# First products ordered by operand at two heads, and the norms' factors loaded in the program's first part

## The reference, cut to what matters

```python
def rms_norm(x, g):
    xf = x.astype(jnp.float32)
    y = xf * lax.rsqrt(jnp.mean(xf * xf, axis=-1, keepdims=True) + EPS)
    return (y * g.astype(jnp.float32)).astype(x.dtype)

def first_block(x, norm_pre, norm_post, ...):
    for i in range(DEPTH):
        h = rms_norm(x, norm_pre[i])
        ...
        x = x + rms_norm(y, norm_post[i])
    return x
```

## Time and profile before

| | us |
|---|---|
| median of three runs | 3822.8 |
| lowest and highest | 3817.92 and 3824.0 |
| the profiled execution's own time | 3820.23 |
| its span, first to last instruction | 3818.7 |
| PE busy | 3637.5 (95%) |
| DVE busy | 1873.1 (49%) |
| ACT busy | 1238.3 (32%) |

### The profile page before, as it was taken

One profiled execution on the slowest core, in us unless ns is written; L12 is line 12 of the kernel. 1 busy time (PEld: TensorE's weight loads), 2 busy tenths in 40 slices (PEclk: granted clock), 3 DMA queues, 4 the chain that ended last, 5 costly groups with the idle time before them and its releaser, 6 DMA issues. The chain is left out here.

```text
span 3818.7 us, 48925 instructions
## 1 busy us (share of the span) xinstructions
PE 3637.5 (95%) x18270; PEld 2939.1 (77%) x18270; DVE 1873.1 (49%) x3663; ACT 1238.3 (32%) x2411; POOL 130.8 (3%) x142
## 2 busy tenths in 40 slices
PE   8999999989999999999998899999958999999999
PEld 6888888857777777777777687677947777887887
DVE  4244244363333454555555544544675657644443
ACT  3243123133323333332323434443232333233222
POOL 0000010000000000000000100000010000000000
PEclk9999999999999999999999999999979999999999
DMA  4222242221111212211111320111222322232223
GB/s 144 98 85 66 64 130 69 88 91 58 52 57 38 73 54 63 58 53 46 45 46 50 112 107 26 40 48 57 87 104 89 100 80 86 73 113 94 99 94 121
DMA packets 134070, 292.16 MB, mean 77 GB/s; under 512 B 31217, under 2 KB 69665, under 8 KB 133777
## 3 DMA queue, kind: packets, MB, share of 16 engines
q1 hardware_dynamic: 117024, 248.03, 19.7%
q0 software_dynamic: 14768, 33.49, 2.9%
q10 hardware_dynamic: 2112, 8.39, 0.6%
HBM read 244.23 MB, written 51.85 MB: 78 GB/s over the span
## 5 line engine op out<-in xcount | busy, mean ns | idle before, releaser
L142 DVE TENSOR_TENSOR all_w_lo<-all_w_raw,all_w_hi 128x1024 fp32r<-128x1024 f32 x311 | 380.6, 1224 | 293.1 <-ACT all_w_hi L137 292.4
L137 ACT ACTIVATE all_w_hi<-all_w_raw 128x1024 fp32r<-128x1024 f32 x311 | 326.7, 1051 | 508.2 <-PE om_z L152 261.4
L1076 PE MATMUL da_z<-all_hi,all_w_hi 128*128 128x512 f32 x736 | 305.7, 415 | 4.1 <-DVE all_w_lo L142 4.1
L1076 PE MATMUL da_z<-all_hi,all_w_lo 128*128 128x512 f32 x736 | 291.3, 396 | 0.0
L1076 PE MATMUL da_z<-all_lo,all_w_hi 128*128 128x512 f32 x736 | 289.8, 394 | 0.0
L152 PE MATMUL om_z<-all_hi,all_w_hi 128*128 128x512 f32 x640 | 257.2, 402 | 7.5 <-DVE all_w_lo L142 4.4
L945 ACT ACTIVATE da_pt<-da_tr 128x512 f32<-128x512 f32 (+1 forms) x192 | 101.0, 526 | 486.3 <-PE da_tr L1129 486.3
L152 PE MATMUL om_z<-all_hi,all_w_lo 128*128 128x512 f32 x640 | 255.4, 399 | 0.0
L953 ACT ACTIVATE at_p<-at_logit,da_pair_max 128x256 f32<-128x256 f32 (+1 forms) x384 | 178.0, 465 | 238.4 <-DVE da_pair_max L1332 238.1
L152 PE MATMUL om_z<-all_lo,all_w_hi 128*128 128x512 f32 x640 | 253.7, 396 | 0.0
L152 PE MATMUL pr_g<-all_hi,all_w_hi 128*128 128x344 f32 (+1 forms) x624 | 212.2, 340 | 10.3 <-issue 4.9
(11 more groups left out here) (569 smaller groups left out, 7509.4 us busy)
## 6 DMA issues: line engine op xcount, KB each, us to landing
all_w_raw<-in_w_mlp SPq DMA_DIRECT2D x128, 512.0 KB, 3.4
all_w_raw<-in_w_ug SPq DMA_DIRECT2D x48, 512.0 KB, 4.2
all_w_raw<-in_w_qkv SPq DMA_DIRECT2D x48, 512.0 KB, 3.6
all_w_raw<-in_w_in SPq DMA_DIRECT2D x27, 512.0 KB, 3.6
da_w_raw<-in_w_qkv SPq DMA_DIRECT2D x24, 512.0 KB, 3.5
all_w_raw<-in_w_bo SPq DMA_DIRECT2D x24, 512.0 KB, 3.4
all_w_raw<-in_w_v SPq DMA_DIRECT2D x20, 512.0 KB, 4.0
vhat<-ag_vst ACTq DMA_DIRECT2D x4, 2048.0 KB, 7.3
```

Of the source, the lines that this page charges most:

```text
L137: self.nc.scalar.activation(self.hi[b][:, :], self.raw[b][:, :], ACT.Copy).then_inc(self.hi_done[b], 1)
L142: self.nc.vector.tensor_tensor(self.lo[b][:, :], self.raw[b][:, :], self.hi[b][:, :].bitcast(F32), ALU.subtract).then_inc(self.lo_done[b], 1)
L1076: last = nc.tensor.matmul(z[h][:, :], wp[u][:, ws], ap[:, kk, cols], start=(kk == 0 and m == 0), stop=(kk == KT - 1 and m == 2))
```

## The change

Three things. In ag, the first 12 products (k = 0 of unit 0) are ordered by operand: first the four with both upper halves, after a wait for `w_hi` and `hi[0]` only; then the four with `w_lo`; then the four with `lo[0]`. In da the 12 products of k = 0 of the first two weight units are ordered the same way, followed by the 6 of the third. And the four factor tiles `post0`, `pre1`, `post1`, `pre2` are kept for the whole program and loaded by SP in ag, behind `ln_b`, with a wait of SP for their landing; the four loads at the heads of da and pr and the waits for them are gone.

```diff
@@ gmlp, sync
             sp.dma_start(ln_b[:, :], a["ln_b"].rearrange("(j p) -> p j", p=P), allow_slow_non_contiguous=True).then_inc(s_lnp, 16)
+            for name, t in norms.items():
+                sp.dma_start(t, a[name]).then_inc(s_norms, 16)
+            sp.wait_ge(s_norms, 16 * len(norms))
             for u in range(2, len(v_units)):
                 load_v(u)
@@ gmlp, tensor
+                w.upper(pe, b, n)
+                wk = [t[b][:, :].rearrange("p (u k f) -> p k u f", u=4, k=2) for t in (w.hi, w.lo)]
+                if u == 0:
+                    pe.wait_ge(s_hi, 1)
+                    for m in ms:
+                        nc.tensor.matmul(bank[m][:, :], hi[:, 0, m * P:m * P + P], wk[0][:, 0], start=True, stop=False)
                 w.split(pe, b, n)
-                wk = [t[b][:, :].rearrange("p (u k f) -> p k u f", u=4, k=2) for t in (w.hi, w.lo)]
                 for k2 in range(2):
                     k = 2 * kp + k2
+                    if k == 0 and u == 0:
+                        for m in ms:
+                            nc.tensor.matmul(bank[m][:, :], hi[:, 0, m * P:m * P + P], wk[1][:, 0], start=False, stop=False)
+                        pe.wait_ge(s_lo, 1)
+                        for m in ms:
+                            nc.tensor.matmul(bank[m][:, :], lo[:, 0, m * P:m * P + P], wk[0][:, 0], start=False, stop=False)
+                        continue
@@ dilated_attention, sync
-            sp.dma_start(post[:, :], a_in["post0"]).then_inc(s_gain, 16)
-            sp.dma_start(pre[:, :], a_in["pre1"]).then_inc(s_gain, 16)
@@ dilated_attention, scalar; vector has the same
-            act.wait_ge(s_gain, 32)
@@ dilated_attention, tensor
+            pe.wait_ge(s_hi, 1)
+            for u in range(2):
+                w.split(pe, u, 0)
+            for m, (wp, ap) in enumerate(((w.hi, hi), (w.lo, hi), (w.hi, lo))):
+                if m == 2:
+                    pe.wait_ge(s_lo, 1)
+                for u in range(2):
+                    for h in range(2):
+                        nc.tensor.matmul(first[u][h][:, :], wp[u][:, 0:P], ap[:, 0, halves[h]], start=m == 0, stop=False)
+            w.split(pe, 2, 0)
             for k in range(KT):
                 pe.wait_ge(s_lo, k + 1)
-                for u in range(3):
-                    if k == 0:
-                        w.split(pe, u, 0)
+                for u in (range(3) if k else (2,)):
@@ projection_and_sticks, sync
-            sp.dma_start(post[:, :], a["post1"]).then_inc(s_norm, 16)
-            sp.dma_start(pre[:, :], a["pre2"]).then_inc(s_norm, 16)
@@ projection_and_sticks, scalar; vector has the same
-            act.wait_ge(s_norm, 32)
@@ the whole program
+        norms = {n: top.sb(n, [P, KT])[:, :] for n in ("post0", "pre1", "post1", "pre2")}
```

More of the change, by code:

```diff
@@ L146, in split, with upper @@
         pe.wait_ge(self.lo_done[b], self.uses[b] + n + 1)
+    def upper(self, pe, b, n):
+        pe.wait_ge(self.hi_done[b], self.uses[b] + n + 1)
     def products(self, out, b, act_hi, act_lo, cols, ks=range(KT)):
@@ L177, in over_same_bytes, with gmlp @@
         return t
-def gmlp(nc, a, w, hi, lo, x_kept, inv, vhat, vecs, tiles, ident, ones, yo):
+def gmlp(nc, a, w, hi, lo, x_kept, inv, vhat, vecs, tiles, ident, ones, yo, norms):
     heads, down = A_HEADS // 2, KT // 2
@@ L678, in attention_tiles, with dilated_attention @@
         return q, k_, v, bias, logit, p
-def dilated_attention(nc, a_in, w, hi, lo, x_kept, yo, over_yo, inv, inv_post, x_out, bias_dram, o_dram, lse_dram, lead, lead_sum, ident, ones):
+def dilated_attention(nc, a_in, w, hi, lo, x_kept, yo, over_yo, inv, inv_post, x_out, bias_dram, o_dram, lse_dram, lead, lead_sum, ident, ones, post, pre):
     turns = 3 * B_PAIRS
@@ L707, in dilated_attention @@
         pt.append(st.sb("pt1", [P, 512]))
-        post = st.sb("post", [P, KT])
-        pre = st.sb("pre", [P, KT])
         eps = st.sb("eps", [P, 1])
@@ L741, in dilated_attention @@
             st.sem(x) for x in ("qs", "vt", "vts", "qk_s", "max", "exp", "t", "pt_s", "pv_s", "rden_s", "o_s", "keep", "bias_s", "odma", "zero", "l", "ldma"))
-        s_free, s_ident, s_gain, s_eps, s_m, s_xp, s_hi, s_lo, s_sq, s_acc, s_tot, s_ln, s_inv, s_kept = (
-            st.sem(x) for x in ("gate_read", "ident_in", "gain_in", "eps_s", "m_s", "xp", "hi_s", "lo_s", "sq_s", "acc_s", "tot_s", "ln_s", "inv_s", "kept"))
+        s_free, s_ident, s_eps, s_m, s_xp, s_hi, s_lo, s_sq, s_acc, s_tot, s_ln, s_inv, s_kept = (
+            st.sem(x) for x in ("gate_read", "ident_in", "eps_s", "m_s", "xp", "hi_s", "lo_s", "sq_s", "acc_s", "tot_s", "ln_s", "inv_s", "kept"))
         s_lnd, s_share, s_lns, s_merge, s_before, s_stored, s_turned, s_yt = (
@@ L1672, in over_x_tiles, with projection_and_sticks @@
     return vt, dt, sd
-def projection_and_sticks(nc, a, w, hi, lo, inv, x, x_again, x_out, over_x, keep, table, cst, proj, conv, o_cat, ident, ones):
+def projection_and_sticks(nc, a, w, hi, lo, inv, x, x_again, x_out, over_x, keep, table, cst, proj, conv, o_cat, ident, ones, norms):
     units = [U_SQ, U_SK, U_SV, U_SQ + 1, U_SK + 1, U_SV + 1, U_DT] + list(range(U_X, U_X + 8)) + [U_Z, U_Z + 1, U_Z + 2, U_Z + 3,
@@ L1726, in projection_and_sticks @@
         gains = st.sb("gains", [P, 2])
-        post = st.sb("post", [P, KT])
-        pre = st.sb("pre", [P, KT])
+        post, pre = norms["post1"], norms["pre2"]
         eps = st.sb("eps", [P, 1])
@@ L1745, in projection_and_sticks @@
         begin = (g, [zb[0], zb[1], ob[0]])
-        (s_norm, s_par, s_table, s_m, s_xp, s_hi, s_lo, s_sq, s_acc0, s_tot, s_ln, s_inv, s_eps, s_zero, s_zout) = (
-            st.sem(n) for n in ("norm", "par", "table_in", "m_s", "xp", "hi_s", "lo_s", "sq_s", "acc0", "tot_s", "ln_s", "inv_s", "eps_s", "zero_s", "zero_out"))
+        (s_par, s_table, s_m, s_xp, s_hi, s_lo, s_sq, s_acc0, s_tot, s_ln, s_inv, s_eps, s_zero, s_zout) = (
+            st.sem(n) for n in ("par", "table_in", "m_s", "xp", "hi_s", "lo_s", "sq_s", "acc0", "tot_s", "ln_s", "inv_s", "eps_s", "zero_s", "zero_out"))
         (s_mm, s_ev, s_psq, s_blk, s_pb, s_r, s_nrm, s_vt, s_cm, s_cx, s_cl, s_ce, s_out, s_cc) = (
@@ L3095, in build @@
         x = yo = top.sb("yo", [P, KT, T])
-        gmlp(nc, a, w, hi_t, lo_t, x_kept, inv_t, vhat, vecs, tiles, ident, ones, yo)
+        gmlp(nc, a, w, hi_t, lo_t, x_kept, inv_t, vhat, vecs, tiles, ident, ones, yo, norms)
         with Stage(nc, "mixers") as st:
@@ L3100, in build @@
             x_again = dilated_attention(nc, a, w, hi_t, lo_t, x_kept, yo, over_yo, inv_t, inv[:, META:], x_dram, tiles, o_dram, lse_dram, lead,
-                                        lead_sum[:, :], ident, ones)
+                                        lead_sum[:, :], ident, ones, norms["post0"], norms["pre1"])
             c = st.sb("cst", [P, total - late])
@@ L3105, in build @@
             keep = {name: st.sb(name, shape).ap() for name, shape in shapes.items()}
-            projection_and_sticks(nc, a, w, hi, lo, inv, x, x_again, x_dram, over_x, keep, (c[:, :], a["cst"][:, late:total]), cst, proj, conv, o_cat, ident, ones)
+            projection_and_sticks(nc, a, w, hi, lo, inv, x, x_again, x_dram, over_x, keep, (c[:, :], a["cst"][:, late:total]), cst, proj, conv, o_cat, ident, ones,
+                                  norms)
             gated_recurrence(nc, proj, a["hg_gain"], cst, keep, FIRST, hi_f, x, x_dram, o_cat)
```

3 lines of the change are left out of this document (1 added, 2 removed).

## The result

| | before | after |
|---|---|---|
| median of 15 runs, us | 3826.29 | 3831.6 |
| lowest and highest | 3817.92 and 3831.33 | 3828.79 and 3836.09 |
| the profiled execution's own time | 3820.23 | 3831.74 |
| its span | 3818.7 | 3830.2 |

The ratio of the change to before is 1.0017, interval 1.001 to 1.0025: slower by 6.5 us (3.8 to 9.6); the two medians alone differ by 5.3. Of the miss of 9.4 us, 3.5 are the baseline: I anchored on the median of three runs, 3822.8, and the median of fifteen is 3826.29.

The account below looks back on a forecast made before the run. PE, busy 95% of the span, was taken as the bound, so edits pay only where it idles. Terms +2.5 (ag) - 2.35 (da) - 0.7 (pr) = -0.55 us against the 3822.8 us median gave 3822.2 us, range 3817 to 3828.

Parts of the forecast that it names:

- The order of products: Heads of ag and da: PE's first products start sooner, but later waits remain, so worth nothing.
- da, -2.35 us: Head of da: without the load DVE's chain and all behind it start 2.35 us sooner (1.9 to 2.56).
- the two waits left there: Head of da: ACT waits 0.4 us for the third buffer's weights; half is covered, leaving DVE 0.2 us.
- Rival 2: da's gains don't come through because PE or ACT's split bounds it: +1.8 us, 3824.6 us; chance 0.17.
- PE's idle 2.40 us ahead of k = 1: Head of da: if a pause of some 2 us lowered the clock, the later k's slack would absorb it.
- ag, +2.5 us (1.4 to 5.6): Head of ag: SP's loads and wait delay the third weight unit 2.1 us, plus 0.4 us of slower clock.
- the last goes out at 18.3: Head of ag: SP issues four small loads from 16.98 us at 0.43 us a step, the last at 18.3.
- The clock term: Head of ag: a 1.2 GHz stretch behind PE's longer stop before the third unit costs 0.4 us net.
- pr, -0.7 us: Head of pr: DVE's earlier start removes PE's 0.54 us stop and some slower restart: -0.7 us (0 to -1.3).
- DVE can start then: Head of pr: DVE starts once POOL's first product is there, about 2191.2 us, 0.8 us before 2192.02.
- The lower bound, 0: Head of pr: no gain at all, if PE is the bound throughout.

Follow-up runs that it names:

- e3: Kernel before with only the new order of PE's first products in ag and da; ratio to before 1.0001.
- e1: The change with SP's wait for the four factor loads moved to the end of ag, loads left in place; ratio to before 1.0018.
- e12: The change with SP's wait moved to the end of ag and 128 unused bytes behind the factor tiles (weights 256 bytes on); ratio to before 1.0013.
- e2: The change with the four factor loads issued late in ag, beside x_kept's, and the wait behind them; ratio to before 1.0014.
- e10: The whole change with 128 unused bytes behind the factor tiles, so weights lie 256 bytes on; ratio to before 1.0019.
- e13: The same kernel as e10, timed again on another chip; ratio to before 1.0002.
- e4: Kernel before plus one unused tile of 128 bytes a partition ahead of the weight tiles, no instruction differing; ratio to before 1.0015.
- e7: Kernel before plus an unused tile of 256 bytes a partition ahead of the weight tiles; a single execution, 3833.94 us.
- e14: The same kernel as e7, timed with 11 executions; ratio to before 1.0000, median 3823.01 us.

## Why the prediction was wrong

**The order of products: nothing.** Right, shown by e3 at both heads.

**da, -2.35 us.** Right: 2.2 us by rows of the change itself, 2.0 to 2.4 in every version with the factors loaded in ag, and the two waits left there, 0.59 and 0.29 us, are those I named. Rival 2 falls. PE's idle 2.40 us ahead of k = 1 was taken up by the later k, as said.

**ag, +2.5 us (1.4 to 5.6): the mechanism right, the size too small.** It measured 5.3 us in the change's profile, 2.7 and 5.5 in two of the version with padding. The release came 3.4 us later, not 2.1: "the last goes out at 18.3" missed that the first small load pays the 1.2 us that the place behind ln_b costs whoever stands there, and ln_b's own issue took 10.05 us. e1 splits it: some 1.2 us for the wait and 2.2 for the issues. The clock term, put at 0.4, came to 1.9 us, which is what is left of the 5.3: two stretches of 3.4 us at 1.2 GHz, up to 1.7 us lost in each, with 1.1 hidden. I had foreseen one stretch at most; the second, behind a stop of 1.85 us, I had excluded because one of 1.72 us had gone by without. The stops do not decide this by their length alone: behind 3.18 us (e1) and 3.02 (e12) no slow stretch came, behind 2.86 (e2), 3.69 (e10) and 4.26 one did, and a stop of 1.89 us in e1 had none behind it where 1.81 us in e13 had one. The Trainium skill (TensorE: Matmul & The Clock Gate, HAM oscillation) tells of a kernel in which waits for DMA of some 3 to 5 us were each followed by slow products; the stops of 3.69, 4.26 and 4.94 us agree with that, those of 3.02 and 3.18 don't, and it tells of no slow products behind stops as short as 1.81, 1.85 and 2.86 us, which were followed by some here.

**pr, -0.7 us.** Wrong: 0. DVE did start 0.7 us sooner, but then more of it ran beside POOL's second product and it took 0.71 us longer, to end as late as before; PE's stop that was to go is still there. The step that failed is "DVE can start then": it could, and won nothing. The lower bound, 0, held by luck, since its reason was PE as the bound.

The sum with measured terms is +5.3 - 2.2 + 0 + 3.2 = +6.3 us, beside 6.5 (3.8 to 9.6) by the ratio. That ag's 5.3 comes from one execution and may well be 3 in another is its weak point: with 3.3 the sum is 4.3, still in the interval. That the sum comes so near to 6.5 is in part luck: e4's 5.7 us at an unchanged mean clock say that placement costs more than the 3.2 us of the rounds, and where the rest stands isn't shown. The profiles' spans differ by more, 11.5 us. Stretches at 0.50 in the later parts come and go between executions of one kernel (the spans of e7 and e14, the same kernel, are 3832.4 and 3828.5), so the 6.2 us by which the parts behind pr's head are longer in the change's profile are no part of the explanation.

By these numbers the whole change with its placement repaired should stand about 1 us above before (3.3 - 2.2); e13 (1.0002) fits, e10 and e12 don't, and what they lose besides is time at the lower clock.

No version here beats the kernel before beyond doubt. The best is the factors alone, loaded late in ag with the weights 256 bytes on: 0.9992 and 1.0002.

## What to carry to other kernels

A new tile at the front of the memory plan is an edit to everything behind it: before a small loss is put down to the new instructions, run the old kernel with an unused tile of that size, and try other sizes. A load that is moved to a busy queue pays the price of its place there, not that of its size, and a wait right behind it stops all that is urgent. And where effects are 0.1%, time the same kernel twice before explaining a result, and compare the mean granted clocks: here two timings of one kernel, on two chips, lay 0.17% apart, and nearly all of it was time at the lower clock.

## What the runs showed of the hardware

- PE's pace in float32 products of 128 x 512 depends on where the operands lie: 1149.2 us for the stretch of 48 common and 22 own weight units in da with the weight tiles at 0 or 256 bytes of shift, 1151.7 at 64 and 1152.4 at 128, at a clock of 1.00 throughout. At 128 bytes that is 2 ns in a product with `w_hi` and nothing in one with `w_lo`. Activations moved against unmoved weights cost 5 ns in a product of the last part (389 to 394).
- The issue of a DMA of 4 KB took 0.43 us on a free queue and 1.00 to 1.17 us right behind ln_b, whose own issue held SP for 9.1 to 10.1 us.
- DVE's addition of 128 x 512 took 0.74 us with POOL idle, 0.97 us with 0.44 us beside POOL's product and 1.68 us with 1.12 us beside it. It ended 3.05 to 3.07 us behind POOL's start in eighteen profiles, whenever it began.
- Stops of PE of 1.81, 1.85 and 2.86 us in ag were followed by stretches at 1.2 GHz of 3.4 us. Others there, of 1.89, 3.02 and 3.18 us, were not.
